# Prompt attention: VectorE's second head on GpSimd in the last two pairs, values in front of scores on TensorE

## What is computed

```python
# heads 0..7: forgetting attention
sc = einsum("bqhd,bkhd->bhqk", q, k) * scale + c[q] - c[k]     # c: running sum of log f
sc = where(k_pos <= q_pos, sc, -inf)
p = softmax(sc); o = einsum("bhqk,bkhd->bqhd", p, v)
# heads 8..15: dilated attention with a relative-position bias; the kernel adds the
# bias and the mask as one 128x512 tile for each head, then does the same softmax
```

## Time and profile before

| | |
|---|---|
| median of 3 runs | 1701.33 us (1699.52 to 1702.0) |
| profiled execution | 1705.38 us, its span 1703.8 us |
| busy, share of the span | PE 95%, DVE 80%, ACT 46%, POOL 34% |
| granted clock of TensorE, mean | 0.983 of full |
| prompt attention | from 192 to 282 us of the span |

### The profile page before, as it was taken

How to read it: one execution, slowest core, us unless ns; L and a number is a source line. 1 busy time by engine, 2 the same in 40 slices (tenths; PEclk the granted TensorE clock), 3 DMA queues, 4 the chain that set the end, 5 groups by cost and what they waited for, 6 DMA issues and landing times.

```text
span 1703.8 us, 27739 instructions
## 1 busy us (share of the span) xinstructions
PE 1623.8 (95%) x9666; PEld 1461.8 (86%) x9666; DVE 1360.3 (80%) x3159; ACT 776.4 (46%) x1262; POOL 579.9 (34%) x513
## 2 busy tenths in 40 slices
PE   5999987797999999989999999999999999999997
PEld 4999744497999999989999999997888888888886
DVE  4224585354899999979999999997999999999996
ACT  4222374223434433367767777763333333333334
POOL 0000380002544534654334334433343333433320
PEclk9999997997999999999999999999999999999999
DMA  3342562712333423499999999999999999999991
GB/s 119 106 156 94 164 198 98 271 73 78 130 131 109 135 100 107 158 354 371 388 369 397 382 370 388 404 404 389 404 403 399 404 405 399 404 403 399 404 365 53
DMA packets 158620, 463.52 MB, mean 272 GB/s; under 512 B 18224, under 2 KB 64432, under 8 KB 154546
## 3 DMA queue, kind: packets, MB, share of 16 engines
q1 hardware_dynamic: 98930, 248.59, 39.7%
q0 software_dynamic: 50944, 178.96, 27.5%
q10 hardware_dynamic: 8640, 34.61, 5.0%
HBM read 406.12 MB, written 57.63 MB: 272 GB/s over the span
## 4 chain that ended last, share of the span: by engine, by line
PE 47%; DVE 21%; DMA 3%; issue 3%; ACT 1%; POOL 1%; another core or an unknown queue 0%; SPq 0%; DVEq 0%; ACTq 0%; POOLq 0%
PE va L230 10%; PE va L231 10%; PE va L232 10%; PE hp L230 4%; PE hp L231 4%; PE hp L232 4%; DVE gathered L1396 3%; DVE og L1901 3%; DVE ulo L1912 2%; PE ggp L1841 2%; DVE vw L1396 2%; DMA hidden_values<-gelu_out 1%; DVE sc L1606 1%; DVE oh L1900 1%; DVE X L1605 1%
## 5 line engine op out<-in xcount | busy, mean ns | idle before, releaser
L230 PE MATMUL hp<-mid_hi,uhi 128*128 128x384 f32 x1024 | 354.6, 346 | 9.1 <-issue 3.5
L231 PE MATMUL hp<-mid_lo,uhi 128*128 128x384 f32 x1024 | 345.2, 337 | 0.0
L232 PE MATMUL hp<-mid_hi,ulo 128*128 128x384 f32 x1024 | 343.8, 336 | 0.0
L230 PE MATMUL va<-vhi,ahi 128*128 128x512 f32 x768 | 299.7, 390 | 3.4 <-DVE hid L1396 2.7
L231 PE MATMUL va<-vlo,ahi 128*128 128x512 f32 x768 | 299.5, 390 | 0.0
L232 PE MATMUL va<-vhi,alo 128*128 128x512 f32 x768 | 299.4, 390 | 0.0
L1771 POOL DMA_INDIRECT gathered<-in_v_experts,eidx x160 | 175.0, 1094 | 311.6 <-DVE acc L2221 222.8
L1309 POOL TENSOR_TENSOR ulo<-uw,uhi 128x1024 fp32r<-128x1024 f32 x49 | 124.1, 2533 | 261.0 <-ACT uhi L1305 261.0
L230 PEld LDWEIGHTS hp<-mid_hi,uhi 128*128 128x128 f32 x1024 | 193.2, 189 | 14.5 <-issue 5.6
L232 PEld LDWEIGHTS hp<-mid_hi,ulo 128*128 128x128 f32 x1024 | 193.3, 189 | 0.0
L231 PEld LDWEIGHTS hp<-mid_lo,uhi 128*128 128x128 f32 x1024 | 193.1, 189 | 0.0
(11 more groups left out here) (314 smaller groups left out, 3413.1 us busy)
## 6 DMA issues: line engine op xcount, KB each, us to landing
uw<-in_u_experts SPq DMA_DIRECT2D x128, 512.0 KB
vw<-in_v_experts SPq DMA_DIRECT2D x68, 512.0 KB
more_v<-in_v_experts SPq DMA_DIRECT2D x60, 512.0 KB
gate_matrix<-gst ACTq DMA_DIRECT2D x12, 2048.0 KB
hidden_values<-gelu_out SPq DMA_DIRECT2D x72, 192.0 KB
hd_mid<-hidden_values SPq DMA_DIRECT2D x8, 1536.0 KB
gt_mid<-gate_matrix SPq DMA_DIRECT2D x8, 1536.0 KB
hd_freed<-hidden_values SPq DMA_DIRECT2D x7, 1536.0 KB
```

What stands on the lines that cost most here:

```text
L230: nc.tensor.matmul(out, a_hi, b_hi, start=first, stop=False)
L231: nc.tensor.matmul(out, a_hi, b_lo, start=False, stop=False)
L232: return nc.tensor.matmul(out, a_lo, b_hi, start=False, stop=last)
```

## The change

From step 24 on (`SHARED = 6 * QB`, pairs 6 and 7) VectorE normalizes only head 0 of `E`, and GpSimd normalizes head 1, after the reciprocal (`inverted`) and after its own copies for the sample queries (`sam["qd"]`). It counts its passes in a new semaphore, `halved`, and TensorE waits for it between the two heads of a turn. In the same steps VectorE, not ScalarE, copies head 1's turned tiles also for the two widest steps of a pair. In all pairs `values` of the pair before now stands in front of `scores(s + 3)` on TensorE.

```diff
@@ -658,11 +658,13 @@
             FOX = PAIRS // 2
+            SHARED = 6 * QB
+            halved = sem("a_halved")
             def kept_by_scalar(s, u):
-                return u == 0 or s % QB >= QB - 2
+                return u == 0 or s < SHARED and s % QB >= QB - 2
@@ -703,6 +705,14 @@
                 spread_queries(0)
+                for s in range(SHARED, STEPS):
+                    n = (s % QB + 1) * P
+                    pool.wait_ge(inverted, s + 1)
+                    if s == SHARED:
+                        pool.wait_ge(sam["qd"], 8)
+                    else:
+                        pool.wait_ge(halved, s - SHARED)
+                    nc.gpsimd.tensor_scalar(E[:, s % RE, 1, :n], E[:, s % RE, 1, :n], rden[:, s, 1:2], None, ALU.mult).then_inc(halved, 1)
@@ -768,6 +778,8 @@
                     for u in range(2):
+                        if u and s >= SHARED:
+                            pe.wait_ge(halved, s - SHARED + 1)
                         for k in range(s % QB + 1):
                             cols = slice(k * P, (k + 1) * P)
                             last = nc.tensor.transpose(TE[u][:, cols], E[:, s % RE, u, cols], ident[:])
@@ -791,10 +803,10 @@
                 for s in range(STEPS):
                     turn(s)
+                    if s and s % QB == 0:
+                        values(s // QB - 1)
                     if s + 3 < STEPS:
                         scores(s + 3)
-                    if s and s % QB == 0:
-                        values(s // QB - 1)
                 values(PAIRS - 1)
@@ -826,7 +838,7 @@
                     n = (s % QB + 1) * P
-                    for u in range(2):
+                    for u in range(2 if s < SHARED else 1):
                         last = nc.vector.tensor_scalar(E[:, s % RE, u, :n], E[:, s % RE, u, :n], rden[:, s, u:u + 1], None, ALU.mult)
                     last.then_inc(weighed, 1)
```

## The result

| | before | after |
|---|---|---|
| median | 1701.33 us (9 runs, 1699.52 to 1704.9) | 1707.65 us (9 runs, 1704.54 to 1711.37) |
| ratio after / before | | 1.003, 95% interval 1.002 to 1.004 |
| profiled execution, its span | 1705.38, 1703.8 us | 1710.32, 1708.8 us |
| granted clock, mean | 0.983 | 0.978 |

A forecast was written before the change was run, and what follows sets the result against it. A loop of waits in the prompt attention, VectorE without slack, was taken as the bound. The main case summed swap +2.66 and GpSimd part -0.3 to +2.4 us on 1701.33: 1703.7 us, range 1700.0 to 1707.5.

The forecast's parts named there:

- The bound, and that the loss passes on whole: Prompt attention, 90 of 1703.8 us: a loop of waits with no engine full; changes at its end pass on whole.
- The swap: Values before widest scores in all pairs: VectorE's maxima start later, 3.83 us behind the pair's first turn; +2.66 us in total.
- 6.78 us are left: VectorE's remaining work from the widest step's maxima to the next pair's turn, 7.12 us less a 0.34 wait; period 10.61.
- The GpSimd part: Pairs 6 and 7: head 1 normalized by GpSimd, its widest copies moved to VectorE; -0.3 us, bounds -0.6 and +0.9.
- DVE's balance is nothing: Pairs 6 and 7: VectorE gives up some 1.2 us of weights and takes over copies costing it 1.1 us.
- ACT gets 1.0 us of slack: ScalarE, relieved of head 1's widest copies, gains 1.0 us, helping only in the last pair's tail.
- the last copies run on two engines at once: 0.5 us less: Tail of the last pair: final copies run on two engines at once, saving 0.5 us.
- the 0.2 us for the widest step: Widest step: the second head's turn comes some 0.2 us late, waiting for GpSimd's pass; nothing in the other steps.
- The port rival: GpSimd takes the shared memory entry first, VectorE's half waits the whole pass in eight steps: +3.1 us, 1706.8; chance 0.12.
- The swap pays: Scores ready when VectorE is free, saving its 0.72 us copy wait per pair: 5.0 us over seven pairs, 1696.3; chance 0.08.
- the clock stay up at the end: Shorter rest before step 31 keeps PE's clock at full; 2.7 us come back, 1701.0, no change; chance 0.10.
- The clock falls inside the pairs: Two PE rests per pair become one of 1.7 us and a short one; one more fall costs 2.7 us, 1706.4; chance 0.12.

The follow-up runs named there:

- the swap alone: Kernel before with only `values` of the pair before put in front of `scores(s + 3)`, no GpSimd pass, ScalarE's copies kept: 1704.62 us against 1703.38, ratio 1.0007.
- the copies alone: Kernel before with head 1's two widest copies of pairs 6 and 7 on VectorE, no GpSimd pass: 1705.43 us, ratio 1.0013.
- the new kernel with filled rests: Kernel after plus ten idle TensorE transposes behind the second turn of each pair: 1701.73 us against 1704.33 for the kernel before, ratio 0.9986.

## Why the prediction was right or wrong

**The bound, and that the loss passes on whole.** Right: the loop of waits decides, and the next stage followed in 43.27 us as before.

**The swap: +2.66 us, measured 1.9** (1.8 in pairs 1 to 6 and 0.1 at the end). The mechanism was right at each place it named: the maxima start at 3.80 us (3.83 forecast), ACT's wait is 0.59 us (0.6), the turn of step 4j+2 stands 262.94 - 256.82 = 6.12 us behind the first (about 6.5; with one head less on VectorE here, and 274.97 - 268.48 = 6.49 in the swap alone). The period without GpSimd is 10.31 us against 10.61. The term that was off is "6.78 us are left": from the maxima's start to the next first turn are 267.05 - 260.54 = 6.51 us. Until the reciprocal of the widest step it was 3.32 us before (261.25 - 257.93) and is 2.84 with the swap. The 0.34 us of waiting went, as counted, and with it some 0.08 us at the read-out that had stood before the wait and 0.06 us in front of the reciprocal of 384 columns; the last 0.13 us are in shorter distances between the rows behind. In the pairs with the causal product the three loops grew by 0.16, 0.14 and 0.45, where 0, 0.34 and 0.56 stood: the sum of these (0.75 against 0.90) was nearly right, the places were not. The wait of "about 1 us" in front of the maxima is 2.05: the copy ahead of them starts 1.46 us behind the pair's first turn now and 2.53 before, so the wait grew at both of its ends, without a cost.

**The GpSimd part: -0.3 us, measured about +1.0.** This is the step that failed, at "DVE's balance is nothing". With transposes in both kernels, pair 6 takes 11.11 us against 10.31, and the end takes 15.47 (against 15.28 in the swap alone at full clock). The balance of busy time may well be nothing; what counted is the place. The order printed ahead of the prediction shows the copy of 512 columns behind the next step's weights and in front of the maxima. The next pair's turn needs the weights and also the freed tiles of that copy, so where ScalarE had done that copy beside VectorE's weights, now one engine does both in turn: 1.03 us of wait. The copy of 384 columns costs nothing with the scores in front (9.77 us). With the values in front the second wait comes in: VectorE's copy of 384 stands 0.43 us for the turn of head 1, behind GpSimd's pass of 1.47 us. With scores in front that wait is absent, and there the whole GpSimd part costs 0.44 us of pair 6 and not 0.80. The rows put most of the difference down to this wait; no run tests it by itself. "ACT gets 1.0 us of slack" bought nothing, and "the last copies run on two engines at once: 0.5 us less" did not come either: the end grew by 0.2. In the sum the 0.2 us for the widest step stands once, though both pairs have one; with it twice the term is -0.1.

The pass itself was mis-sized. With the scores in front that had no effect on the time; with the swap it is in the wait of 0.43 us above. The groups of GpSimd's passes after (busy us, mean ns | idle):

```profile
L715 POOL TENSOR_SCALAR E<-E,rden 128x512 f32<-128x512 f32 x2 | 3.1, 1565 | 0.3 <-POOL E L715 0.3
L715 POOL TENSOR_SCALAR E<-E,rden 128x384 f32<-128x384 f32 x2 | 2.9, 1468 | 6.2 <-DVE rden L838 6.2
L715 POOL TENSOR_SCALAR E<-E,rden 128x256 f32<-128x256 f32 x2 | 2.2, 1082 | 2.5 <-DVE rden L838 2.5
L715 POOL TENSOR_SCALAR E<-E,rden 128x128 f32<-128x128 f32 x2 | 1.4, 694 | 5.8 <-DVE rden L838 5.8
```

512 columns take 1.56 us, or 1.85 when released at the same moment as VectorE's half: above the upper bound of 1.27. The Trainium skill (GPSIMD Engine Reference, section 3.1, Elementwise) states 769 ns for 512 elements in a tight unrolled loop, its best case. The trace shows twice that for this pass, and the measurement decides.

**The port rival (1706.8, chance 0.12).** It did not happen: VectorE's half took 0.49 and 0.53 us beside GpSimd's pass, not the pass's length more. As expected, the one that took longer was GpSimd. **The swap pays (0.08)** did not happen either: the maxima waited for the scores. Nor did the clock stay up at the end of the profiled execution (0.10): the turn at 276.10 took 1.74 us.

**The clock falls inside the pairs (1706.4, chance 0.12).** This one came on top of the main case. The argument against it, "its rests stay below those in front of 272.99", was wrong by the prediction's own figure: the new rest in front of the turn of 4j+2 was forecast and measured at 1.7 us, at least as long as the 1.65 of the earlier trace rows. But the length of the rest does not decide by itself, as the falls behind shorter rests show. The two falls cost 11.77 - 10.77 and 11.36 - 10.38, 1.0 us each, and in the other kernels up to 1.7 (10.10 against 8.41 us in the copies alone), not 2.7. A likely reason, not tested by itself, is that turns wait for VectorE anyhow and hide part of the slower products. The price of 2.7 us was taken from the end, where nothing else runs; there it is right: 17.77 - 15.16 = 2.6.

**The sum.** 1.9 (swap) + 1.0 (GpSimd part) = 2.9 us, against +2.4 forecast, and 2.0 for the two falls of the profiled execution, 0.2 more at the end: 5.1 of the 5.16 us. The medians' differences are 3.3 and 6.3 us. The first is near the 2.9 without any fall; the second would take two or three falls more than the kernel before has, or the spread of 3 us that the kernel before shows between measurements, and the record does not tell which. Shown: that the new kernel with filled rests had no fall in its profile, and that this brings 5.9 us in the median, about half of it at the end of the stage. With transposes in both, the new kernel is 1.97 us over the one before (1701.73 and 1699.76). How often the falls strike in each kernel was not measured, since one execution of each is profiled. That the swap makes them likelier rests on the rest of 1.7 us and on the profiles without idle transposes: two falls in each of the three with the swap, none, none, none, one, one, two and two in the seven without it (the one with transposes in its last pair only among them). It is not settled. When after was measured again, one of its two falls took pair 0, in front of which no values had moved.

## What to carry to other kernels

When work moves from one engine to another, do not balance the busy sums: look at which instruction now stands in front of the one that the bound loop waits for. A copy of 0.68 us that had run beside other work cost 0.44 us of a pair, and a pass of 1.85 us placed off that path cost nothing. The same pass came onto the path once the order had changed, and the two together cost 0.8. And where TensorE rests in a stage, look at the granted clock behind the rests; filling them with idle transposes is cheap, and here it was worth more than the whole rearrangement. Follow the gain into the next stage, where a faster engine may only wait longer.

## What was unexpected of the hardware

GpSimd's multiplication of fp32 by one value for each partition took 0.69, 1.08, 1.47 and 1.85 us for 128 to 512 columns when it started with VectorE's pass, 3 ns a column, near its two-operand subtraction (2.53 us for 1024) and not its fill (1.06 us for 1152). The 512 columns took 1.56 us when they started 0.42 us behind VectorE's pass. VectorE's own stayed at 0.49 and 0.53.

TensorE's clock fell to half inside a loop in which the engine was busy 59.27 of 70 us. The rests in front of the falls were between 0.7 and 1.7 us, and the same rests were passed without a fall in other pairs and executions. With ten idle transposes a pair the seven periods held 1.00 in both kernels that had them. A fall inside the loop cost 1.0 to 1.7 us; at the end of the stage it cost 2.6. With the swap alone the clock once stayed up at that end behind a rest of 2.09 us.
